# Key and value pages on 64 partitions in runs of 2 KB, and scores as eight TensorE tiles, in the sample stage of a two-layer decoder step

## What is computed

```python
score = jnp.where(valid, imp + jnp.where(forced, FORCE, 0.0), NEG)
top_val, top_idx = lax.top_k(score, min(SEL_TOP, n_sel))       # 16 of 65 blocks of 64 tokens
ks, vs = fetch_sel(top_idx)                                     # from the page pool
s_s = jnp.einsum('btgrd,btgkjd->btgrkj', q, ks) * sc
p_s = masked_softmax(s_s..., mask_s...)
o_s = jnp.einsum('btgrm,btgmd->btgrd', p_s, vs...)
p_w = masked_softmax(jnp.einsum('btgrd,bsgd->btgrs', q, kw) * sc, mask_w)    # window of 512 tokens
o_w = jnp.einsum('btgrs,bsgd->btgrd', p_w, vw)
return g[..., 0, None] * o_c + g[..., 1, None] * o_s + g[..., 2, None] * o_w
```

## Time and profile before

| | |
|---|---|
| median of 3 runs | 1384.14 us |
| profiled execution | 1385.89 us, its span 1384.2 us |
| PE busy | 1244.8 us (90%) |
| DVE, ACT, POOL busy | 485.4, 412.9, 175.3 us |
| mean granted clock of TensorE | 0.93 |
| moved by DMA | 238.01 MB, mean 172 GB/s |

### The profile page before, as it was taken

The page is one execution under the profiler, slowest core; times in us unless marked ns, Lnnn a source line. Parts: engine busy times, 40 slices in busy tenths (PEclk is TensorE's granted clock), DMA queues, the critical chain, the costliest instruction groups (busy, mean ns, idle before and its releaser), DMA issues. The chain is left out here.

```text
span 1384.2 us, 25565 instructions
## 1 busy us (share of the span) xinstructions
PE 1244.8 (90%) x9287; PEld 782.9 (57%) x9287; DVE 485.4 (35%) x1478; ACT 412.9 (30%) x1088; POOL 175.3 (13%) x287
## 2 busy tenths in 40 slices
PE   4899999992986979999999889999999799989996
PEld 1676755751654744747778845555555434444455
DVE  2352120004564240101210175556555433333334
ACT  3311111112220031000101146565556433333443
POOL 0000000001000000000000122222222353343300
PEclk8999999995786989999999589999999999999998
DMA  9414333338003131212300377666666698999972
GB/s 388 171 61 182 122 122 122 122 133 280 24 10 121 61 135 36 74 38 75 125 0 1 110 262 241 223 224 230 224 229 222 231 342 296 329 318 318 339 268 70
DMA packets 94905, 238.01 MB, mean 172 GB/s; under 512 B 11450, under 2 KB 49468, under 8 KB 90300
## 3 DMA queue, kind: packets, MB, share of 16 engines
q1 hardware_dynamic: 74076, 169.26, 35.0%
q0 software_dynamic: 20704, 67.13, 13.5%
HBM read 227.68 MB, written 17.05 MB: 177 GB/s over the span
## 5 line engine op out<-in xcount | busy, mean ns | idle before, releaser
L385 PE MATMUL ps<-arena,wring 128*128 128x288 f32 x1664 | 416.9, 412 | 6.9 <-DMA wring<-in_weights 5.4
L385 PEld LDWEIGHTS ps<-arena,wring 128*128 128x128 f32 x1664 | 318.2, 192 | 100.0 <-issue 8.0
L1520 POOL DMA_DIRECT2D arena<-in_cmp_pages x128 | 70.1, 549 | 489.5 <-issue 278.7
L392 PE MATMUL ps<-wring,arena 128*128 128x512 f32 (+1 forms) x240 | 107.8, 608 | 7.1 <-ACT arena L1220 7.1
L1614 DVE CUSTOM_DVE_ANT_0 wring<-ps,wring 128x128 f32<-128x128 f32 (+3 forms) x128 | 57.6, 488 | 75.8 <-PE ps L1543 74.1
L392 PEld LDWEIGHTS ps<-wring,arena 128*128 128x128 f32 (+1 forms) x240 | 43.4, 184 | 67.5 <-issue 60.3
L1606 ACT ACTIVATE wring<-ps 128x128 f32<-128x128 f32 (+3 forms) x128 | 49.0, 436 | 90.8 <-PE ps L1566 90.8
L2079 DVE CUSTOM_DVE_ANT_1 arena<-ps,small 128x512 f32<-128x512 f32 x64 | 44.3, 693 | 89.7 <-PE ps L1998 89.6
L2055 ACT ACTIVATE arena<-arena 128x512 f32<-128x512 f32 (+1 forms) x88 | 57.0, 649 | 60.1 <-DVE arena L2095 60.1
L1592 ACT ACTIVATE wring<-wring 128x128 f32<-128x128 f32 (+3 forms) x128 | 70.7, 559 | 8.4 <-DVE wring L1614 8.3
L1679 PE MATMUL ps<-arena 128*32 128x256 f32 x1024 | 70.1, 391 | 0.0
(11 more groups left out here) (383 smaller groups left out, 1572.7 us busy)
## 6 DMA issues: line engine op xcount, KB each, us to landing
wring<-in_weights SPq DMA_DIRECT2D x27, 2048.0 KB, 9.0
arena<-in_cmp_pages SPq DMA_DIRECT2D x128, 256.0 KB, 3.5
arena<-in_cmp_pages POOLq DMA_DIRECT2D x128, 256.0 KB, 4.3
wring<-in_kv_pages SPq DMA_DIRECT2D x64, 256.0 KB, 9.3
wring<-in_kv_pages POOLq DMA_DIRECT2D x64, 256.0 KB, 6.8
arena<-in_kv_pages SPq DMA_DIRECT2D x50, 256.0 KB, 6.5
arena<-in_kv_pages POOLq DMA_DIRECT2D x50, 256.0 KB, 6.9
arena<-in_out_tiles SPq DMA_DIRECT2D x12, 512.0 KB, 8.4
```

The lines of the kernel that those rows point to most:

```text
L385: last = pe.matmul(out[:, 0:HT], w[:, k, ct * P:ct * P + P], moving[k][:, half * HT:half * HT + HT], start=(k == 0), stop=(k == KT - 1))
L392: last = pe.matmul(main[0:m, :], moving[k][:, index * P:index * P + m], w[:, k, :], start=(k == 0), stop=(k == KT - 1))
L1520: eng.dma_start(cring[q % CR][:, 2 * half + j, :], v["cmp_pages"][bass.ds(ids[2 * d + j], 1)] .rearrange("o p c -> (o p) c")).then_inc(c_i ...
```

## The change: layout of pages, tiles of the scores, banks

A page keeps its 256 KB but is laid out as 64 partitions: 2 KB of keys (64 features; for each of 4 groups 128 keys) and 2 KB of values (64 tokens of 256, for both halves of the page side by side). A page whose number in its queue's pair is even lands on partitions 0 to 63, an odd one on 64 to 127. The window is laid out in the same order; its DMA stays at 128 partitions.

A score step becomes eight products: for each group (32 columns of query rows) and each half of the partitions ("lane", 64 rows, the features of that one group), 256 moving columns, the keys of two pages. The two lanes write to two banks, 0 and 1 for odd steps, 2 and 3 for even ones. `qblk` needs its queries on both halves, so `dve_select` copies four pieces of 64x32 for each sample. DVE now runs two instructions for a step, each with 256 columns, that write every second run of 64 in `SS`. `drop_all` is written in a new order, by three instructions where one was. The new tokens' keys get a second copy, `knew_odd`, with the other half zero. The out tile moves from bank 0 to bank 7 (`XB`), the transposed result of a sample from bank 1 to bank 5. Bank 5 is also a bank of `pe_turn`, so step 1 of a sample now waits for the gate of the sample before.

```diff
-            dve.tensor_scalar(drop_all[:, n, :], score, 0.0, NEG, ALU.is_ge, ALU.mult).then_inc(dve_c, DC_.one(("sel", n)))
+            for lane in range(2):
+                other, rows = slice(DH - lane * DH, 2 * DH - lane * DH), slice(lane * DH, lane * DH + DH)
+                for gp in range(2):
+                    at = 32 * (2 * gp + lane)
+                    dve.tensor_copy(qblk[other, gp, n, at:at + 32], qblk[rows, gp, n, at:at + 32])
+                dve.tensor_scalar(drop_all[:, n, 0:NSEL - 1].rearrange("p (i l q k) -> p i l q k", i=NG, l=2, q=2)[:, :, lane],
+                                  score[:, 0:NSEL - 1].rearrange("p (i q l k) -> p i l q k", i=NG, l=2, q=2)[:, :, lane],
+                                  0.0, NEG, ALU.is_ge, ALU.mult)
+            dve.tensor_scalar(drop_all[:, n, NSEL - 1:NSEL], score[:, NSEL - 1:NSEL], 0.0, NEG, ALU.is_ge, ALU.mult)\
+                .then_inc(dve_c, DC_.one(("sel", n)))
...
-        def bring(eng, n, i, half, lo, cols, src):
-
-            k, vals, done = keys_home(n, i)[:, lo:lo + cols], values_home(n, i)[:, lo:lo + cols], kv_in[half][(n * NL + i) % KS]
+        def bring(eng, n, i, half, rows, lo, cols, src):
+
+            k, vals, done = keys_home(n, i)[rows, lo:lo + cols], values_home(n, i)[rows, lo:lo + cols], kv_in[half][(n * NL + i) % KS]
             if vals.offset > k.offset:
                 both = bass.AP(k.tensor, k.offset, [list(k.ap[0]), [vals.offset - k.offset, 2], [1, cols]])
-                eng.dma_start(both, src.rearrange("p (x c) -> p x c", x=2)).then_inc(done, 16)
+                eng.dma_start(both, src).then_inc(done, 16)
             else:
-                eng.dma_start(k, src[:, 0:cols]).then_inc(done, 16)
-                eng.dma_start(vals, src[:, cols:2 * cols]).then_inc(done, 16)
+                eng.dma_start(k, src[:, 0]).then_inc(done, 16)
...
                 for j in range(2):
-                    bring(eng, n, i, half, (2 * half + j) * KVW, KVW,
-                          v["kv_pages"][bass.ds(ids[2 * d + j], 1)].rearrange("o p c -> (o p) c"))
+                    bring(eng, n, i, half, slice(j * DH, j * DH + DH), half * 2 * KVW, 2 * KVW,
+                          v["kv_pages"][bass.ds(ids[2 * d + j], 1)].rearrange("o (x p) c -> (o p) x c", x=2))
 
         def load_window(eng, n):
...
+        def score_lanes(i):
+
+            return ps[:, 0:2, 0:KVW] if i % 2 else ps[:, 2:4, 0:KVW]
...
+            if i == 0:
+                pe.wait_ge(dve_c, DC_["sel", n])
-            bank = ps[:, 2 + i % 2, :]
+            lanes = score_lanes(i)
             if i <= NG:
-                for gp in range(2):
-                    if i < NG:
-                        keys = keys_home(n, i).rearrange("p (q c) -> p q c", q=GP)[:, :, gp * P:gp * P + P]
-                        out = bank[gp * DH:gp * DH + DH].rearrange("p (q n) -> p q n", q=GP)
-                    else:
-                        keys, out = keys_home(n, NG)[:, gp * TP:gp * TP + TP], bank[gp * DH:gp * DH + DH]
-                    last = pe.matmul(out, qblk[:, gp, n, gp * DH:gp * DH + DH], keys, start=True, stop=True)
+                keys = keys_home(n, i).rearrange("p (q g n) -> p q g n", q=2, g=G)
+                for g in range(G):
+                    for lane in range(2):
+                        rows = slice(lane * DH, lane * DH + DH)
+                        out = lanes[32 * g:32 * g + 32, lane].rearrange("p (q n) -> p q n", q=2)
+                        last = pe.matmul(out, qblk[rows, g // 2, n, 32 * g:32 * g + 32], keys[rows, :, g, :], start=True, stop=True)
             else:
                 for x in range(2):
-                    for gp in range(2):
-                        last = pe.matmul(bank[gp * DH:gp * DH + DH, x * NS:x * NS + NS], qblk[:, gp, n, gp * DH:gp * DH + DH],
-                                         knew[:, 2 * x + gp, :], start=True, stop=True)
+                    for g in range(G):
+                        last = pe.matmul(lanes[32 * g:32 * g + 32, 0, x * NS:x * NS + NS], qblk[:, g // 2, n, 32 * g:32 * g + 32],
+                                         (knew, knew_odd)[g % 2][:, 2 * x + g // 2, :], start=True, stop=True)
             last.then_inc(scored, 1)
...
             pe.wait_ge(exped, n * NJ + at + 1)
+            if n and at == 1:
+                pe.wait_ge(so_gated, n)
             if n * NJ + at >= 2:
...
-            if i < NG:
-                keep = drop_all[:, n, 8 * i:8 * i + 8].unsqueeze(2).to_broadcast([P, 8, 64])
-                dve.tensor_tensor_reduce(SS[:, i * TP:i * TP + TP].rearrange("p (k n) -> p k n", k=8), bank.rearrange("p (k n) -> p k n", k=8),
-                                         keep, -1.0, 3.0e38, ALU.add, ALU.min, mxs[:, i:i + 1]).then_inc(kept, 1)
-            elif i == NG:
-                dve.tensor_tensor_reduce(SS[:, SWIN:SWIN + TP], bank, cd("win_add"), -1.0, 3.0e38, ALU.add, ALU.min,
-                                         mxs[:, NG + 1:NG + 2]).then_inc(kept, 1)
+            if i <= NG:
+                o, m = (i * TP, 2 * i) if i < NG else (SWIN, 2 * NG + 1)
+                for lane in range(2):
+                    if i < NG:
+                        add = drop_all[:, n, 8 * i + 4 * lane:8 * i + 4 * lane + 4].unsqueeze(2).to_broadcast([P, 4, DH])
...
-                last = pe.matmul(ps[:, 0, :], tile_w[:, k, :], zT[:, k, 0:TP], start=(k == 0), stop=(k == KT - 1))
+                last = pe.matmul(ps[:, XB, :], tile_w[:, k, :], zT[:, k, 0:TP], start=(k == 0), stop=(k == KT - 1))
...
-            pe.transpose(ps[:, 1, 0:P], oS[:, n % 2, :], ident).then_inc(so_turned, 1)
+            pe.transpose(ps[:, 5, 0:P], oS[:, n % 2, :], ident).then_inc(so_turned, 1)
...
+                dve.memset(knew_odd[0:DH], 0.0)
+                dve.tensor_copy(knew_odd[DH:P], knew[DH:P])
+                dve.drain()
+                dve.memset(knew[DH:P], 0.0)
...
+def kv_pages(k, vals):
+
+    n = k.shape[0]
+    k = k.transpose(0, 3, 2, 1).reshape(n, DH, G * P)
+    vals = vals.reshape(n, 2, DH, KVW).transpose(0, 2, 1, 3).reshape(n, DH, 2 * KVW)
+    return np.concatenate([k, vals], axis=1)
```

46 lines of the change are left out of this document (28 added, 18 removed).

## The result

The changed kernel takes 1483.03 us (median of 4 runs, 1480.68 to 1484.82), the kernel before beside it 1386.73 us (median of 4). The ratio is 1.0687, with a 95% interval of 1.0654 to 1.0721: it is slower by about 96 us. The profiled execution has a span of 1479.0 us. The prediction of 1364 us was wrong in sign, and the result lies outside its range. Rival 1 has the right mechanism, though not its size.

A forecast was written before the change was run, and what follows sets the result against it. The prediction took the samples' stage to be bound by DMA by a small margin, PE next. It summed loads -18, scores -4, additions +1 and +1 to -20 us, forecasting 1364 us; the range was 1350 to 1435 us.

The forecast's parts named there:

- Rival 1: Page writes: 64 partitions may have half the ways into SBUF; slower, 1395 to 1450 us, likeliest 1425; chance 0.34.
- The loads: Page DMAs in the samples' stage: runs of 2 KB save 13 us, shorter pauses 5 us, together -18 us.
- PE now frees its homes earlier: DMA pauses, mostly behind an out tile, 10 us in all: half of them saved, 5 us.
- only part of that appears: Rival 1's slowdown of page loads: of +12.4 us a sample, +4 to +12 us taken, since engines mix the halves.
- The estimate from the figures of the Trainium skill: Page loads, if its port rule held in full: 40 us for a sample's pages, above 1470 us in all.
- The scores: PE's score steps: 0.55 us instead of 1.01; worth -4 us in the last sample with scores, nothing in DMA-bound ones.
- What is added: Extra work on DVE and PE: +1 us for DVE and selection, +1 us for the gate wait.
- DVE's pair: Two DVE instructions a score step: about 0.85 us in place of 0.77, covered by DVE's idle time.
- The wait for the gate: Step 1's transposes on PE come 0.6 us later; costs only in the last samples, +1 us.
- The selection: Six more short DVE instructions in the last selection ahead of the first out tile, 0.2 us each: +1 us.
- Rival 2: Page loads: the longer runs don't pay, memory holds the engines back; no change, 1377 us; chance 0.10.
- rival 3: PE's scores: the eight tiles don't run at once; above 1500 us, or about 1415 with two at a time; chance 0.04.

The follow-up runs named there:

- f_tiles_128: The changed kernel's eight tiles with the page transfers of the kernel before (128 partitions, runs of 1 KB): 1400.53 us, ratio 1.0097.
- a_128x2k: The changed kernel with each page brought to all 128 partitions in one run of 2 KB: 1394.76 us, ratio 1.0048.
- b2_before_2k: The kernel before with each page brought to all 128 partitions in one run of 2 KB instead of two of 1 KB: 1369.49 us, ratio 0.9896.
- l2_half_columns: The kernel before with each score product over 256 of its 512 columns, half the keys' scores left out: 1397.15 us, ratio 1.0055.

## Why the prediction was wrong

**The loads, -18 us; the step that failed.** The term was right for what it named: longer runs by themselves measured -15 us. It gave the 64 partitions no cost and left them to rival 1, and these cost 83 us (before's scores) to 88 us (eight tiles). I had put 0.52 on the forecast because of the earlier trace rows, 434 GB/s in a microsecond with stores from 64 partitions among others. That reading failed: 36 of 101 packets there were of 2 KB, and the 44 of 8 KB and more held some 0.35 of the 0.43 MB; they must be the store of `kk`, issued right behind that of `vv_s` (1152 KB and 128 KB), which reads all 128 partitions. A burst of such stores alone moves 194 GB/s. The text said "a mixture" and then let it weigh as evidence. The 5 us of the term that "PE now frees its homes earlier" was to save in pauses didn't come either: with the tiles the DMA engines' share went from 0.96 to 0.92 (f_tiles_128) and 0.89 (a_128x2k).

**Rival 1, 1395 to 1450 us: right mechanism, mis-sized.** Two steps failed. "While SP's and POOL's current pages lie in different halves nothing is lost": opposite and equal halves move the same 232 GB/s, and the kernel with opposite halves takes 1482 us. And "only part of that appears": all of it does. Eight samples of 9.96 MB at 233 in place of 321 GB/s are 342 in place of 248 us, 94 us more, against 87 measured. The estimate from the figures of the Trainium skill, 40 us for a sample's pages and above 1470 us in all, came nearest: from one out tile to the next are 41.7 us on the mean, and the whole takes 1483.

**The scores, -4 us: wrong in sign.** The size of the edit was right (0.59 us, predicted 0.55). The step that failed is "In the DMA-bound samples this only makes PE's idle stretch longer and is worth nothing". With the step shortened alone the kernel measured +8 us. There the idle time did grow, but by 4.3 us a sample where the scores saved 3.2, and what PE does besides took 1.7 us more at the lower clock. For the last sample the term was right in kind: it is 3.2 us shorter there. With the eight tiles it is 3.1 us longer instead, and 4.8 us in the changed kernel, since the stalls of TensorE, which the prediction doesn't have, take more than the scores give.

**What is added, +2 us.** DVE's pair is hidden, and shorter than predicted (0.77 us, as one instruction of 512 columns took before, not 0.85): its second instruction starts while the first one's accumulator is read. The wait for the gate was right in size (0.71 us) and worth nothing by itself. The selection was mis-sized: I charged its six instructions once, ahead of the first out tile, but the compressed branch's stage has DVE's selection on its path in every sample, 0.8 us each, 6 us in all.

**Rival 2** (the longer runs don't pay) is refuted by b2_before_2k, **rival 3** (the tiles don't run at once) by the 0.59 us.

**The sum by what was measured.** The tiles with all that comes with them +13 (f_tiles_128), the longer runs -6 in that kernel (a_128x2k), the half partitions +88: in all 95, measured 96. These are differences from one kernel to the next, so that they add up proves nothing. The 13 can't be split into 8 for the shorter scores and 5 for the rest, since f_tiles_128 loses by stalls what l2_half_columns loses by waits.

## What to carry to other kernels

Before a transfer is narrowed to 64 partitions, look at which ones: 0 to 63 take about 200 GB/s where all 128 take 320, two queues bring that to 232 only, and a high DMA share hides it, so read the rate beside the share. Where loads and TensorE are nearly even, shortening TensorE's steps can make the kernel slower, here by 8 us with the columns halved and by 13 with the tiles; ask what the freed time will be spent on, and whether many short products leave TensorE waiting for its instructions. Weigh a row that is a mixture as no evidence, and measure the disputed rate by itself.

## What the runs showed of the hardware that was not expected

- 64 partitions from 16 or 48 are as slow as one half (199 and 198 GB/s), those from 32 and the even ones are not (287 and 274), and 32 partitions alone reach what their half does (192 and 197).
- Eight tiles of 64 x 32 run at once: 16 recorded matmuls of 256 columns in 0.59 us. Two column halves of 128 x 64 do too, so one of them alone takes as long as both (1.00 us).
- At 52 recorded matmuls in 1.77 us TensorE stalls, mostly for 1 to 3 us, and goes on 1.2 to 1.6 us after a fetch of 16 KB of instructions has landed (78 of 78 stalls of 0.85 us or more in nine kernels), with the DMA engines 0.61 or 0.92 busy alike. At 52 in 2.7 us it doesn't.
- Cutting a product of 512 columns into four of 128 costs time: 1.51 us for a step's scores in place of 1.01.
